# A ring of eight half size weight units, and six of them for token tile 0 ahead of tile 1

## The chip, the cores and the metric

The kernel runs on one core of one Trainium2 chip. The metric is the device time of one execution in microseconds (us); the number compared is the median of several runs.

## The reference

A transformer of three blocks on 256 tokens of width 1024, in float32. Everything is a chain of RMS norms, projections and small attentions:

```
h = x
layer 0: y = norm(h); y = [window attention (8 heads, rope, sinks) | HGRN2 (4 heads, blocks of 32)] @ w_out
layer 1: y = norm(h); y = chunk attention (16 heads, relative bias) @ w_out
both:    h = h + norm(y)
         y = (gelu(conv3(norm(h) @ w_u)) * (norm(h) @ w_v)) @ w_down      # 1024 -> 2816 -> 1024
         h = h + norm(y)
block 2: y = norm(h); three attentions of y (causal with rope; forgetting; over 256 memory rows)
         h = h + (sum of sigmoid(gate_b) * (attention_b @ w_b)) @ w_out
         h = h + (silu(norm(h) @ w_gate) * (norm(h) @ w_up)) @ w_down
```

The inputs of each projection are the whole output of the norm ahead of it, and each norm needs a full row (1024 features) of the projection ahead of it. There are 256 tokens, so each engine sees two tiles of 128 tokens, tile 0 and tile 1.

## The kernel before, in words

**Weights.** All weights are laid out on the host as 172 units of 128 partitions x 2048 columns (1 MB; UNIT = 2048, line 45; STREAM, line 49, lists the stages in their order with the number of units, the blocks of 128 input features in a unit and the columns). SyncE loads them in this order into a ring of RAW = 4 slots `raw` (line 411), waiting for the semaphore unit_used, which counts the units that TensorE has finished. ScalarE rounds each unit into `hi` (round_unit, line 508), VectorE subtracts to get the rest `lo` (split_unit, line 1136), and TensorE takes three products for each block: hi with the rounded activations, hi with their rest, lo with the rounded ones. So a unit passes through four engines: load, rounding, split, matmuls.

**Two kinds of product.** Token-major stages (tokens_by, tokens_unit; matmuls at line 790, 128 x 512) have 128 tokens as rows of PSUM, two banks a tile. A unit holds two blocks of 128 input features with 1024 columns, so a unit is 12 matmuls for tile 0 and 12 for tile 1. Feature-major stages (features_of; line 848, 128 x 256) have features as rows and both tiles as columns: q and k, the gates and the up projections. These need the activations of both tiles from the first matmul on.

**Order by hand.** Each engine's program is one fixed list. `units(n)` on ScalarE and VectorE means: round (split) all units up to n here. Whatever stands behind it in the list waits for it, and it waits for the load.

**The end of a projection and the next entry.** Six projections are TAILS: even_out, down0, odd_out, down1, merge_out, down2. Their last two units go as a pair: both units for tile 0 (then the semaphore tile_done), then both for tile 1. With tile_done VectorE and ScalarE begin on tile 0. norms_between is what they do behind the first four: the norm of the projection's output (weigh_product, square_product), its sum into h (add_product, line 1200), the squares and weights of the sum (square_sum, weigh), the scaling (scale, line 1181), then the transposed halves are rounded (turned_hi, line 546) and their rest taken (turned_lo, line 1187). GpSimd makes the reciprocal roots in between (lines 436 and 438). TensorE transposes the normed rows of a tile with `turn` (line 859), two semaphored halves of four transposes each.

On TensorE a token-major stage is entered by `enter`: turn tile 0, one unit for tile 0, turn tile 1 (`entry(1)`), the second unit for tile 0, then both units for tile 1. The feature-major up stages turn both tiles and then start. FEATURE_MAJOR (stages 3, 6 and 8) are up0, up1 and up2; stages 4 and 7 are odd_v and moba_qk; stages 2 and 5 are the entries to even_out and odd_out behind attentions; stage 0 is mem_kv. The core of VectorE's list between two norms:

```
weigh_product(g, 0, base, tile_done, ...)
units(last(name) + 1)
add_product(g, p, 0)
weigh(g + 1, 0, ...)
weigh_product(g, 1, base, unit_used, last(name))
scale(g + 1, 0)
```

Behind merge_out there is no norm of the product: add_residual (line 1231), squares, weigh, scale, turns.

Of the kernel before, what the change touches and what calls it, by code (L numbers as in the profile page):

```python
# [28 lines left out]
P = 128  # L29
S = 256  # L30
NT = S // P
D = 1024
KD = D // P
FF = 2816
# [10 lines left out]
UNIT = 2048  # L45
RAW = 4
# [3 lines left out]
    ("mem_kv", 4, 2, 1024),  # L50
    ("even_a", 4, 2, 768), ("even_qf", 4, 8, 256), ("even_ig", 4, 2, 1024), ("even_out", 4, 2, 1024),
    ("up0", 22, 8, 256), ("down0", 11, 2, 1024),
    ("odd_v", 4, 2, 1024), ("odd_qk", 8, 8, 256), ("odd_out", 4, 2, 1024),
    ("up1", 22, 8, 256), ("down1", 11, 2, 1024),
    ("moba_qk", 4, 2, 1024), ("both_v", 4, 2, 1024), ("fox_qk", 4, 2, 1024), ("mem_q", 3, 3, 520),
    ("gates", 12, 8, 256), ("branches", 6, 4, 512), ("merge_out", 4, 2, 1024),
    ("up2", 22, 8, 256), ("down2", 11, 2, 1024),
# [5 lines left out]
WIDTH[FIRST["mem_q"] + 2] = 2 * 520  # L63
# [12 lines left out]

TAILS = ["even_out", "down0", "odd_out", "down1", "merge_out", "down2"]
# [50 lines left out]
def lay_out(a):  # L128

    def rows(w, cols, k_of_unit):  # L130

        w = w[:, cols].reshape(-1, P, w[:, cols].shape[1])
        out = []
        for k0 in range(0, w.shape[0], k_of_unit):
            out.append(w[k0:k0 + k_of_unit].transpose(1, 0, 2).reshape(P, -1))
        return out

    def columns(w, groups):

        return [w[:, g].reshape(-1, P, len(g)).transpose(1, 0, 2).reshape(P, -1) for g in groups]  # L140

    r = np.arange
    pairs = [r(256 * j, 256 * j + 256) for j in range(4)]
    two = [np.concatenate([r(P * j, P * j + P), FF + r(P * j, P * j + P)]) for j in range(KF)]
    even, odd, w2 = a["even_w_in"][0], a["odd_w_in"][0], a["w_in_2"][0]
    u = rows(a["w_mem_kv_2"][0], r(1024), 2)

    heads = np.concatenate([r(HD * x, HD * x + HD) for p in range(4) for x in (p, 4 + p)] + [r(512, 768)])
    u += rows(even, heads, 2) + columns(even, [768 + g for g in pairs]) + rows(even, r(1792, 2816), 2)
    u += rows(a["even_w_out"][0], r(D), 2)  # L150
    u += columns(a["ffn_w_up"][0], two) + rows(a["ffn_w_down"][0], r(D), 2)
    u += rows(odd, r(2048, 3072), 2)
    u += columns(odd, [np.concatenate([r(P * j, P * j + P), D + r(P * j, P * j + P)]) for j in range(8)])
    u += rows(a["odd_w_out"][0], r(D), 2)
    u += columns(a["ffn_w_up"][1], two) + rows(a["ffn_w_down"][1], r(D), 2)
    u += rows(w2, r(1024), 2) + rows(w2, np.concatenate([r(1024, 1536), r(2560, 3072)]), 2)
    u += rows(w2, r(1536, 2560), 2) + rows(w2, r(3072, 3592), 3)
    u += columns(w2, [3592 + r(256 * j, 256 * j + 256) for j in range(12)])
    for name in ("w_br_moba_2", "w_br_fox_2", "w_br_mem_2"):
        u += columns(a[name][0], [r(512), r(512, 1024)])  # L160
    u += rows(a["w_out_2"][0], r(D), 2)
    gate_up = np.concatenate([a["w_gate_2"][0], a["w_up_2"][0]], 1)
    u += columns(gate_up, two) + rows(a["w_down_2"][0], r(D), 2)
# [22 lines left out]
def build(nc, dram, out):  # L186
    with ExitStack() as ctx:
# [133 lines left out]
        q_made = sem("q_made")  # L321
# [76 lines left out]
        def _(sp):  # L398
# [3 lines left out]
            for n in range(RAW):  # L402
                if n == 1:
                    sp.dma_start(mem_x[:, 1, :], dram["mem"][P:S, :]).then_inc(mem_in[1], 16)
                if n == 2:
                    sp.dma_start(h[:, :, :], dram["x"].rearrange("(t p) d -> p t d", p=P)).then_inc(x_in, 16)
                sp.dma_start(raw[:, n, :], dram["weights"][n]).then_inc(raw_in[n], 16)
            with sp.Fori(0, UNITS // RAW - 1) as i:
                for s in range(RAW):
                    sp.wait_ge(unit_used, RAW * i + s + 1)  # L410
                    sp.dma_start(raw[:, s, :], dram["weights"][RAW * i + (RAW + s)]).then_inc(raw_in[s], 16)
            for t in range(NT):
# [87 lines left out]
        def _(act):  # L500
# [75 lines left out]
            def feed_forward(layer):  # L576
# [8 lines left out]
                def tile(i, r):  # L585

                    j = 4 * i + r
                    act.wait_ge(unit_used, j + up + 1)
# [5 lines left out]
                    round_unit(j + up + 2, (up + 2 + r) % RAW, i + (up + 2 + r) // RAW, UNIT)  # L594
# [8 lines left out]
                done[0] += KF  # L603
# [4 lines left out]
            units(1)  # L608
            turned_hi(0, 4, h_hi, (0,))
            square_tokens(0, 1, mem_x, (mem_in[1], 16), (mem_in[1], 16))  # L610
            units(2)
# [5 lines left out]
            units(FIRST["even_a"] + 1)  # L617
# [3 lines left out]
            units(FIRST["even_a"] + 2)  # L621
# [3 lines left out]
            units(last("even_a") + 2)  # L625
# [3 lines left out]
            for u in range(4):  # L629
                act.wait_ge(unit_used, FIRST["even_qf"] + u + 1)  # L630
                dst = (hq if u < 2 else hf)[:, 2 * (u % 2):2 * (u % 2) + 2, :].rearrange("p a b -> p (a b)")
                act.activation(dst, bank(u), ACT.Copy if u < 2 else ACT.Sigmoid).then_inc(qf_evac, 1)
                units(FIRST["even_qf"] + u + 3)
            act.wait_ge(f_done, 1)
            act.activation(whole(hf), whole(hf), ACT.Ln).then_inc(ln_done, 1)
            units(FIRST["even_ig"] + 3)
# [3 lines left out]
            units(FIRST["even_ig"] + 4)  # L640
            act.wait_ge(last_done, 1)
            act.activation(whole(hf), whole(hf), ACT.Exp).then_inc(exp3_done, 1)
            units(last("even_ig") + 1)
# [3 lines left out]
            units(last("even_ig") + 2)  # L647
# [963 lines left out]
```

## Time and profile before

| what | value |
|---|---|
| median of 3 runs | 1204.79 us (1204.57 to 1205.15) |
| the profiled execution's own time | 1202.29 us |
| its span | 1200.5 us |
| mean granted TensorE clock | 0.95 |
| PE busy | 1137.8 us (95%), 7452 matmuls |
| weight loads of PE (PEld) | 1032.0 us |
| VectorE (DVE) busy | 703.0 us |
| ScalarE (ACT) busy | 537.6 us |
| GpSimd (POOL) busy | 83.3 us |
| moved by DMA | 194.17 MB, mean 162 GB/s |

PE is a matmul, PEld a weight load into the array, which runs beside the matmuls; SPq is SyncE's queue. A busy PE is not PE at its peak: its rate depends on the granted clock, 1.00 being 2.4 GHz and 0.50 being 1.2 GHz. The span is the part of the profiled execution between the first and the last instruction; 1.8 us of its time lie outside.

### The profile page before, as it was taken

The numbers are of one execution on the slowest core, as the hardware profiler recorded it, in microseconds if no ns is written. First come the engines' busy times: TensorE is split into PE (matmuls) and PEld (weight loads), VectorE is DVE, ScalarE is ACT, GpSimd is POOL, SyncE is SP. The second block draws the span as 40 slices with busy tenths as digits, with TensorE's granted clock in tenths as the row PEclk, the third lists the DMA queues.
The fourth block names the chain that finished last, engine by engine and source line by source line (L and its number), as shares of the span: only waits on it lengthen the run. The fifth ranks groups of instructions, "written<-read, shape, count | busy, mean of one in ns | idle before, by whom it ended". The sixth has DMA issues, their size and how long they took to land.

```text
span 1200.5 us, 18573 instructions
## 1 busy us (share of the span) xinstructions
PE 1137.8 (95%) x7452; PEld 1032.0 (86%) x7452; DVE 703.0 (59%) x937; ACT 537.6 (45%) x743; POOL 83.3 (7%) x113
## 2 busy tenths in 40 slices
PE   5999997999999899879999997999999998999998
PEld 4898676999987689769999886888999987999986
DVE  6567435666653556555666637556555575555542
ACT  5544324554543444434555434435544634444441
POOL 3200002000000201020000002203000000000000
PEclk9998577999999899889999998999999998999999
DMA  7854013555454454244555552554333353555552
GB/s 280 308 180 138 1 51 129 188 192 176 175 200 169 175 173 153 79 173 142 180 186 193 177 195 103 210 202 149 134 114 106 111 193 118 178 183 191 183 180 101
DMA packets 28876, 194.17 MB, mean 162 GB/s; under 512 B 3488, under 2 KB 3680, under 8 KB 6800
## 3 DMA queue, kind: packets, MB, share of 16 engines
q1 hardware_dynamic: 25760, 183.58, 43.9%
q0 software_dynamic: 3056, 9.73, 2.5%
q8 instruction: 45, 0.74, 0.2%
q14 instruction: 15, 0.12, 0.0%
HBM read 192.25 MB, written 1.05 MB: 161 GB/s over the span
## 4 chain that ended last, share of the span: by engine, by line
PE 88%; DVE 5%; ACT 3%; POOL 2%; issue 2%; DMA 1%; DVEq 0%; ACTq 0%; POOLq 0%
PE ps L848 46%; PE ps L790 31%; PE ps L929 3%; PE ps L906 2%; PE ps L859 2%; PE ps L918 1%; DVE xhat L1167 1%; DVE lo L1136 1%; POOL ms L436 1%; PE ps L875 1%; DMA gain<-in_gains 1%; PE ps L974 1%; DVE h L1200 1%; ACT hi L508 1%; DVE y_lo L1187 1%
## 5 line engine op out<-in xcount | busy, mean ns | idle before, releaser
L1136 DVE TENSOR_TENSOR lo<-raw,hi 128x2048 fp32r<-128x2048 f32 (+2 forms) x172 | 389.1, 2266 | 166.9 <-ACT hi L508 166.8
L848 PE MATMUL ps<-y_hi,hi 128*128 128x256 f32 x1504 | 431.2, 287 | 2.0 <-DVE y_lo L1187 2.0
L848 PE MATMUL ps<-y_lo,hi 128*128 128x256 f32 x1504 | 428.4, 285 | 0.0
L848 PE MATMUL ps<-y_hi,lo 128*128 128x256 f32 x1504 | 428.3, 285 | 0.0
L508 ACT ACTIVATE hi<-raw 128x2048 fp32r<-128x2048 f32 (+2 forms) x172 | 323.5, 1887 | 137.3 <-DMA raw<-in_weights 131.2
L848 PEld LDWEIGHTS ps<-y_hi,hi 128*128 128x128 f32 x1504 | 291.5, 194 | 4.1 <-issue 3.7
L848 PEld LDWEIGHTS ps<-y_lo,hi 128*128 128x128 f32 x1504 | 291.6, 194 | 0.0
L848 PEld LDWEIGHTS ps<-y_hi,lo 128*128 128x128 f32 x1504 | 291.3, 194 | 0.0
L790 PE MATMUL ps<-hi,h_hi 128*128 128x512 f32 x328 | 102.6, 394 | 2.0 <-DVE h_lo L1187 1.2
L790 PE MATMUL ps<-hi,h_lo 128*128 128x512 f32 x328 | 102.6, 394 | 0.0
L790 PE MATMUL ps<-lo,h_hi 128*128 128x512 f32 x328 | 102.1, 393 | 0.0
L790 PE MATMUL ps<-hi,y_hi 128*128 128x512 f32 (+2 forms) x288 | 91.6, 399 | 3.1 <-DVE y_lo L1187 2.2
L790 PE MATMUL ps<-lo,y_hi 128*128 128x512 f32 (+2 forms) x288 | 88.9, 390 | 0.0
L790 PE MATMUL ps<-hi,y_lo 128*128 128x512 f32 (+2 forms) x288 | 88.1, 387 | 0.0
L590 ACT ACTIVATE sc<-ps,conv 128x256 f32<-128x256 f32 x44 | 24.9, 565 | 131.3 <-PE ps L848 131.3
L790 PEld LDWEIGHTS ps<-hi,h_hi 128*128 128x128 f32 x328 | 61.5, 189 | 16.6 <-DVE h_lo L1187 1.6
L790 PEld LDWEIGHTS ps<-hi,h_lo 128*128 128x128 f32 x328 | 61.9, 189 | 13.5
L790 PEld LDWEIGHTS ps<-lo,h_hi 128*128 128x128 f32 x328 | 61.9, 189 | 13.3
L859 PE MATMUL ps<-ident,xhat 128*128 128x128 f32 x144 | 29.5, 374 | 44.0 <-DVE xhat L1181 41.6
L790 PEld LDWEIGHTS ps<-hi,y_hi 128*128 128x128 f32 x288 | 54.9, 198 | 16.0 <-DVE y_lo L1187 3.8
L436 POOL TENSOR_SCALAR ms<-ss 128x1 f32<-128x1 f32 x22 | 20.0, 909 | 686.6 <-ACT sc L528 651.5
L859 PEld LDWEIGHTS ps<-ident,xhat 128*128 128x128 f32 x144 | 24.1, 193 | 49.1 <-DVE xhat L1181 34.4
(237 smaller groups left out, 1046.2 us busy)
## 6 DMA issues: line engine op xcount, KB each, us to landing
raw<-in_weights SPq DMA_DIRECT2D x172, 1024.0 KB, 4.8
gain<-in_gains POOLq DMA_DIRECT2D x11, 512.0 KB, 5.4
bias<-in_rel POOLq DMA_DIRECT2D x16, 128.0 KB, 2.4
mem_x<-in_mem SPq DMA_DIRECT2D x2, 512.0 KB, 6.8
h<-in_x SPq DMA_DIRECT2D x1, 1024.0 KB, 13.9
out<-h SPq DMA_DIRECT2D x2, 512.0 KB, 2.6
pick<-in_c_pick POOLq DMA_DIRECT2D x1, 512.0 KB, 8.0
head_gain<-in_head_gains POOLq DMA_DIRECT2D x1, 256.0 KB, 7.9
```

The lines of the kernel that those rows point to most:

```text
L436: pool.tensor_scalar(ms[:, g % 2, t:t + 1], ss[:, g % 2, t, 0:1], ss[:, g % 2, t, 1:2], EPS, ALU.add, ALU.add).then_inc(scaled_ms, 1)
L508: act.activation(hi[:, s, :w], raw[:, s, :w], ACT.Copy).then_inc(hi_done, 1)
L590: act.activation(sc[:, r % 2, :S], ps[:, r, :S], ACT.Identity, scale=conv[:, layer, j, 2:3], bias=conv[:, layer, j, 3:4]).then_inc(conv_be ...
L790: mm = pe.matmul(ps[:, base + 2 * t + half_, :cw], x[:, k + kk, tok], w[:, n % RAW, kk * cols + c0:kk * cols + c0 + cw], start=first and k ...
L848: mm = pe.matmul(dst, w[:, s % RAW, at], x(k), start=first and k == 0, stop=final and k == nk - 1)
L859: mm = pe.transpose(ps[:, base + 2 * t + kh, kk * P:(kk + 1) * P], src[:, t, (4 * kh + kk) * P:(4 * kh + kk + 1) * P], ident[:, :])
L875: mm = pe.transpose(ps[:, b, kk * P:(kk + 1) * P], src[:, t, c0 + kk * P:c0 + (kk + 1) * P], ident[:, :])
L906: mm = pe.matmul(dst, q[:, t * P:(t + 1) * P], k[:, :n], start=True, stop=stage != "f")
L918: mm = pe.transpose(ps[:, 2 + a % 2, i * P:(i + 1) * P], pr[:, a % 2, i * P:(i + 1) * P], ident[:, :])
L929: mm = pe.matmul(place(stage, hh, t), pt[:, a % 2, i * P:(i + 1) * P], v(kt), start=kt == 0, stop=kt == kts[-1])
L974: mm = pe.matmul(ps[:, 5 + b % 3, hh * P:(hh + 1) * P], kend[r, b // 4, hh * P:(hh + 1) * P], hv[r, b // 4, hh * P:(hh + 1) * P], start=Tr ...
L1136: dve.tensor_tensor(lo[:, s, :w], raw[:, s, :w], hi[:, s, :w].bitcast(F32), ALU.subtract).then_inc(lo_done, 1)
```

## The change

It has four parts.

1. Units are half as wide and the ring has twice as many slots: UNIT = 1024, RAW = 8. A token-major unit is now one block of 128 input features with 1024 columns, 6 matmuls a tile; a feature-major one is 128 columns for all 8 blocks. 344 units; every wait counts in half units.
2. At the end of each of the six tails, six half units go for tile 0 and then six for tile 1 (TAIL = 6; before, two whole ones, four halves). At the entries to odd_v and moba_qk six half units go for tile 0 before tile 1 (LEAD = 6); mem_kv has four, even_out and odd_out two, being what their tails leave of eight.
3. `turn_next`: the transposes of tile 0 for the next stage are issued on TensorE ahead of the last half part of tile 1 of the projection, no longer behind it. In a lead, tile 1 is turned ahead of tile 0's last half part.
4. ScalarE's and VectorE's lists between two norms are put in another order, and the feed forward tile rounds and splits one half unit ahead of and one behind its Gelu and product.

The core of the diff:

```diff
-UNIT = 2048
-RAW = 4
+UNIT = 1024
+RAW = 8
+LEAD, TAIL = 6, 6
...
# TensorE, tokens_by
+                def by_tile(first, count, leads, is_tail):
+                    for n in range(first, first + count):
+                        wait_unit(n)
+                        if needs is not None:
+                            pe.wait_ge(*needs(n - n0))
+                        if leads and n == n0 + 4:
+                            pe.wait_ge(y_lo_done, 4 * stage + 2)
+                        if leads and n == first + count - 1:
+                            entry(1)
+                        mm = part(n, 0)
+                    if is_tail:
+                        mm.then_inc(tile_done, 1)
+                    for n in range(first, first + count):
+                        if leads and n - n0 in (0, 4):
+                            pe.wait_ge(y_lo_done, 4 * stage + 3 + (n - n0) // 4)
+                        if is_tail and n == last(name) - 1:
+                            turn_next()
+                        part(n, 1).then_inc(unit_used, 1)
...
+                lead = 4 if name == "mem_kv" else n1 - n0 - TAIL if name in TAILS else LEAD
...
# VectorE, norms_between
                 dve.wait_ge(turned, 4 * stage)
+                units(last(name) + 2)
                 weigh_product(g, 0, base, tile_done, TAILS.index(name) + 1)
-                units(last(name) + 1)
                 add_product(g, p, 0)
                 weigh(g + 1, 0, [h[:, 0, 0:512], h[:, 0, 512:D]])
+                scale(g + 1, 0)
+                units(last(name) + 4)
+                turned_lo(stage, turn_base, y_lo, y_hi, (0,))
                 weigh_product(g, 1, base, unit_used, last(name))
-                scale(g + 1, 0)
...
+                add_product(g, p, 1)
+                weigh(g + 1, 1, [h[:, 1, 0:512], h[:, 1, 512:D]])
+                if stage not in FEATURE_MAJOR:
+                    units(last(name) + 5)
+                scale(g + 1, 1)
+                if stage not in FEATURE_MAJOR:
+                    units(last(name) + 6)
+                turned_lo(stage, turn_base, y_lo, y_hi, (1,))
...
# ScalarE, norms_between
-                units(last(name) + 1)
+                units(last(name) + 2)
                 square_product(g, 0, base, tile_done, TAILS.index(name) + 1)
-                units(last(name) + 2)
                 square_sum(g + 1, 0, p)
+                units(last(name) + 4)
+                turned_hi(stage, turn_base, y_hi, (0,))
                 square_product(g, 1, base, unit_used, last(name))
-                turned_hi(stage, turn_base, y_hi, (0,))
+                if stage not in FEATURE_MAJOR:
+                    units(last(name) + 5)
                 square_sum(g + 1, 1, p)
+                if stage not in FEATURE_MAJOR:
+                    units(last(name) + 6)
                 turned_hi(stage, turn_base, y_hi, (1,))
...
# VectorE, behind merge_out
             add_residual("merge_out", 4, 0)
             weigh(10, 0, [h[:, 0, 0:512], h[:, 0, 512:D]])
-            units(last("merge_out") + 1)
+            scale(10, 0)
+            units(last("merge_out") + 2)
+            turned_lo(8, 4, y_lo, y_hi, (0,))
             add_residual("merge_out", 4, 1)
-            scale(10, 0)
             weigh(10, 1, [h[:, 1, 0:512], h[:, 1, 512:D]])
-            turned_lo(8, 4, y_lo, y_hi, (0,))
+            units(last("merge_out") + 4)
             scale(10, 1)
             turned_lo(8, 4, y_lo, y_hi, (1,))
...
# ScalarE, behind merge_out
             square_sum(10, 0, 4)
-            units(last("merge_out") + 1)
+            units(last("merge_out") + 2)
+            turned_hi(8, 4, y_hi, (0,))
             square_sum(10, 1, 4)
-            turned_hi(8, 4, y_hi)
-            units(last("merge_out") + 2)
+            units(last("merge_out") + 4)
+            turned_hi(8, 4, y_hi, (1,))
...
# ScalarE, feed forward tile (VectorE alike)
-                    round_unit(j + up + 2, (up + 2 + r) % RAW, i + (up + 2 + r) // RAW, UNIT)
+                    round_unit(n + 4, m % RAW, i + m // RAW, UNIT)
                     ... Gelu or Silu ...
+                    round_unit(n + 5, (m + 1) % RAW, i + (m + 1) // RAW, UNIT)
```

In odd_qk, q and k are half units of their own, so q's copy waits for unit_used in place of q_made, and in `tokens_by` merge_out waits for the second half of its input after its fourth half unit.

## Rows read from the trace of the kernel before

**Rows 1.** The page: parts 1 and 4.
```profile
PE 1137.8 (95%) x7452; PEld 1032.0 (86%) x7452; DVE 703.0 (59%) x937; ACT 537.6 (45%) x743; POOL 83.3 (7%) x113
...
PE 88%; DVE 5%; ACT 3%; POOL 2%; issue 2%; DMA 1%; DVEq 0%; ACTq 0%; POOLq 0%
```
**Rows 2.** Waits of PE: line waited for: us in total, times, longest.
```profile
PE ps L859 <- DVE xhat L1181: 41.6, 11, 11.3
```
**Rows 3.** Windows: length, busy us of each engine, clock, DMA share, GB/s.
```profile
188.00:191.60 3.60, 0.03 (x1) 0.00 (x0) 3.57 (x7) 2.76 (x8) 1.30 (x3) 1.00 1.00 380
403.80:406.30 2.50, 2.50 (x8) 2.02 (x7) 1.39 (x2) 2.38 (x3) 1.68 (x4) 0.50 0.95 311
205.00:329.00 124.00, 124.00 (x1034) 124.00 (x1033) 82.08 (x104) 63.59 (x84) 0.00 (x0) 1.00 0.52 178
```
**Rows 4.** The chain that ended last: start us, us, what.
```profile
106.17 1.43 ACT hi L508
...
329.25 54.95 PE ps L790 x240
...
404.15 20.40 PE ps L790 x84
```
**Rows 5.** Groups by form: busy us, mean ns, idle before.
```profile
L1136 DVE TENSOR_TENSOR lo<-raw,hi 128x2048 fp32r<-128x2048 f32 x165 | 377.2, 2291 | 162.0 <-ACT hi L508 161.9
L508 ACT ACTIVATE hi<-raw 128x2048 fp32r<-128x2048 f32 x165 | 313.6, 1907 | 133.0 <-DMA raw<-in_weights 126.9 <-PE ps L848 6.1
...
L1187 DVE TENSOR_TENSOR y_lo<-ps,y_hi 128x512 fp32r<-128x512 f32 x32 | 21.5, 689 | 29.9 <-ACT y_hi L546 29.7
...
L1136 DVE TENSOR_TENSOR lo<-raw,hi 128x1536 fp32r<-128x1536 f32 x4 | 7.0, 1755 | 1.6 <-ACT hi L508 1.6
...
L508 ACT ACTIVATE hi<-raw 128x1536 fp32r<-128x1536 f32 x4 | 6.0, 1495 | 1.4 <-DMA raw<-in_weights 1.4
```
**Rows 6.** Timeline, even_out to up0: start us, length us, operation, idle before.
```profile
182.73 1.37 DVE L1167 TENSOR_TENSOR xhat<-ps,gain 128x512 f32<-128x512 f32 x2 [6.75 <-PE ps L790]
...
189.88 1.28 DVE L1167 TENSOR_TENSOR xhat<-ps,gain 128x512 f32<-128x512 f32 x2
...
191.61 1.82 PE L859 MATMUL ps<-ident,xhat 128*128 128x128 f32 x8 [3.58 <-DVE xhat L1181]
...
192.78 1.41 DVE L1200 SCALAR_TENSOR_TENSOR h<-xhat,rstd,h 128x512 f32<-128x512 f32 x2 [0.83 <-POOL rstd L438]
193.47 0.60 ACT L546 ACTIVATE y_hi<-ps 128x512 fp32r<-128x512 f32 x1 [0.26 <-PE ps L859]
...
199.83 0.55 PE L848 MATMUL ps<-y_hi,hi 128*128 128x256 f32 x1 [0.65 <-DVE y_lo L1187]
```
**Rows 7.** Timeline, down0 to odd_v.
```profile
384.32 1.37 DVE L1167 TENSOR_TENSOR xhat<-ps,gain 128x512 f32<-128x512 f32 x2 [7.39 <-PE ps L790]
...
398.64 1.41 DVE L1200 SCALAR_TENSOR_TENSOR h<-xhat,rstd,h 128x512 f32<-128x512 f32 x2
...
402.23 0.88 DVE L1181 TENSOR_SCALAR xhat<-xhat,rstd 128x512 f32<-128x512 f32 x2 [0.84 <-POOL rstd L438]
...
402.77 1.38 PE L859 MATMUL ps<-ident,xhat 128*128 128x128 f32 x8 [2.05 <-DVE xhat L1181]
```
**Rows 8.** Timeline, merge_out to up2.
```profile
992.54 1.29 DVE L1231 TENSOR_TENSOR h<-ps,h 128x512 f32<-128x512 f32 x2 [6.77 <-PE ps L790]
...
993.96 0.61 ACT L528 ACTIVATE sc<-h 128x512 f32<-128x512 f32 x1
...
1003.66 0.87 DVE L1181 TENSOR_SCALAR xhat<-xhat,rstd 128x512 f32<-128x512 f32 x2
...
1006.81 0.55 PE L848 MATMUL ps<-y_hi,hi 128*128 128x256 f32 x1 [0.65 <-DVE y_lo L1187]
```
**Rows 9.** The page's DMA issues: KB each, median us to landing.
```profile
raw<-in_weights SPq DMA_DIRECT2D x172, 1024.0 KB, 4.8
...
out<-h SPq DMA_DIRECT2D x2, 512.0 KB, 2.6
```

More of the change, by code:

```diff
@@ L43 @@
 REL = 128
-UNIT = 2048
-RAW = 4
+UNIT = 1024
+RAW = 8
 STREAM = [
[L50 to L57, printed above, removed]
+    ("mem_kv", 8, 1, 1024),
+    ("even_a", 8, 1, 768), ("even_qf", 8, 8, 128), ("even_ig", 8, 1, 1024), ("even_out", 8, 1, 1024),
+    ("up0", 44, 8, 128), ("down0", 22, 1, 1024),
+    ("odd_v", 8, 1, 1024), ("odd_qk", 16, 8, 128), ("odd_out", 8, 1, 1024),
+    ("up1", 44, 8, 128), ("down1", 22, 1, 1024),
+    ("moba_qk", 8, 1, 1024), ("both_v", 8, 1, 1024), ("fox_qk", 8, 1, 1024), ("mem_q", 8, 1, 520),
+    ("gates", 24, 8, 128), ("branches", 12, 4, 256), ("merge_out", 8, 1, 1024),
+    ("up2", 44, 8, 128), ("down2", 22, 1, 1024),
 ]
@@ L62 @@
     WIDTH += [_k * _c] * _n
-WIDTH[FIRST["mem_q"] + 2] = 2 * 520
 UNITS = len(WIDTH)
@@ L128, in lay_out, with rows, columns @@
 def lay_out(a):
[L130 to L140, printed above, removed]
+    def rows(w, cols):
+        return list(w[:, cols].reshape(-1, P, len(cols)))
+    def columns(w, cols, width=P):
+        return [w[:, cols[c:c + width]].reshape(-1, P, width).transpose(1, 0, 2).reshape(P, -1) for c in range(0, len(cols), width)]
@@ L154, in lay_out @@
[L154 to L158, printed above, removed]
+    u = rows(a["w_mem_kv_2"][0], r(1024))
+    u += rows(even, heads) + columns(even, 768 + r(1024)) + rows(even, r(1792, 2816)) + rows(a["even_w_out"][0], r(D))
@@ L675, in _ @@
             norms_between(4, 1, 4, "down0", 4, 0)
-            units(last("odd_v") + 2)
+            units(last("odd_v") + 4)
             act.wait_ge(unit_used, last("odd_v"))
@@ L793, in tokens_unit, with tokens_by @@
                 return mm
-            def tokens_by(name, base, y, splits=((0, 512), (512, 512)), entry=None, ready=None, before_last=lambda: None, needs=None):
+            def tokens_by(name, base, y, splits=((0, 512), (512, 512)), entry=None, stage=None, before_last=lambda: None, needs=None, turn_next=lambda: None):
                 n0, n1 = FIRST[name], last(name)
-                first_k = [sum(WIDTH[n0:n]) // COLS[name] for n in range(n0, n1)]
                 def part(n, t):
-                    return tokens_unit(name, n, first_k[n - n0], t, base, y, splits)
-                def pair(n, between=lambda: None, halfway=lambda mm: None):
-                    wait_unit(n)
-                    part(n, 0)
-                    between()
-                    wait_unit(n + 1)
-                    halfway(part(n + 1, 0))
-                    for m in (n, n + 1):
-                        if ready is not None and m == n0:
-                            pe.wait_ge(*ready)
-                        part(m, 1).then_inc(unit_used, 1)
-                n = n0
-                if entry is not None:
-                    pair(n, lambda: entry(1))
-                    n += 2
-                    pe.wait_ge(ready[0], ready[1] + 1)
-                tail = n1 - 2 if name in TAILS else n1
@@ L822, in tokens_by @@
+                n = n0
+                lead = 4 if name == "mem_kv" else n1 - n0 - TAIL if name in TAILS else LEAD
+                if stage is not None and lead:
+                    by_tile(n, lead, True, False)
+                    n += lead
+                    pe.wait_ge(y_lo_done, 4 * stage + 4)
+                tail = n1 - TAIL if name in TAILS else n1
                 while n < tail:
-                    if n == n1 - 1:
+                    if n == n1 - 2:
                         before_last()
@@ L1003, in _, with feed_forward @@
             pe.wait_ge(mk_evac, 2)
-            enter(2, 4, "even_out", 0, attended, [2, 2])
-            def feed_forward(layer, stage, base):
+            enter(2, 4, "even_out", 0, attended, [2, 2], turn_next=lambda: turn_normed(3, 4, 0))
+            def feed_forward(layer, stage, base, turn_next=lambda: None):
                 up = FIRST[f"up{layer}"]
-                for t in range(NT):
-                    turn(stage, xhat, base, t, normed, 2 * NORM_OF_TURN[stage] + t + 1)
+                turn_normed(stage, base, 1)
                 def tile(i, r):
@@ L1444, in _ @@
             units(last("even_out"))
-            norms_between(2, 0, 0, "even_out", 3, 4, 2)
+            norms_between(2, 0, 0, "even_out", 3, 4)
             feed_forward(0)
-            norms_between(4, 1, 4, "down0", 4, 0, 3)
-            units(last("odd_v") + 2)
+            norms_between(4, 1, 4, "down0", 4, 0)
+            units(last("odd_v") + 4)
             dve.wait_ge(unit_used, last("odd_v"))
```

256 lines of the change are left out of this document (125 added, 131 removed).

## The prediction

> **What bounds the kernel now.** I read the page first, then PE's waits, then the order of time at the turns from one stage to the next, then the operations by form. TensorE carries 88% of the chain that ended last [rows 1], so only what PE waits for, or what slows PE, can move the time. Of its waits one group matters: the transposes of the normed rows wait for VectorE's scaling, 41.6 us in 11 waits [rows 2], 11.3 of it at the kernel's start. They stand at five places: behind even_out and odd_out (then an up stage, which needs both token tiles), behind down0 and down1 (then odd_v and moba_qk, which can start on tile 0), and behind merge_out. The loads, rounding and splitting of the weights have room: in an up stage PE is busy all 124 us while VectorE is at 82, ScalarE at 64 and the DMA engines at 0.52 [rows 3]. So the sum is made at the five places, and the rest of the ring is weighed only for what it puts in the chain.
>
> **Units of time.** A matmul of 512 columns takes 0.229 us (54.95 us for 240 [rows 4]). A half unit for one tile (a part) is 6 of them, 1.37 us. The change sends tile_done 6 parts before the end of a projection (8.24 us) instead of 4 (5.50 us). Below, T is where PE would end the projection if it never stalled, and times with a plus sign count from tile_done, so T is +5.50 before and +8.24 after.
>
> **Half size operations.** From 1536 to 2048 columns the split grows from 1755 to 2291 ns and the rounding from 1495 to 1907 ns [rows 5]. A line through each pair gives 1.22 us for a split of 1024 columns and 1.08 us for a rounding; two halves cost 0.15 and 0.26 us more than one whole. That is 25 and 45 us over 172 units, hidden behind PE as long as the engines have the room shown above. It shows only where a rounding or split stands in the chain, as the ScalarE rounding at 106.17 us does [rows 4]. The chain has some three such pieces away from the five places: 3 x 0.26, about +0.7 us.
>
> **even_out to up0, odd_out to up1.** Before: VectorE starts on tile 0's product at 182.73, so tile_done is at 182.69; PE turns tile 0 at 191.61 (+8.92), and its first up matmul is at 199.83 [rows 6]. That is T + 11.6. After: the two splits moved ahead of tile 0's product are done before tile_done (their ring slots come free when the tail begins, 8.2 us earlier), so tile 0's chain is as long as before. PE comes to the point of turn_next after 5 parts, at +6.87, and has to wait until about +8.8: **a stall of 1.9 us ahead of the last part** that wasn't there. Eight transposes (0.9) and the last part (1.37) then end at about +11.1, at T + 2.8. Meanwhile VectorE: the scaling ends at +9.2; then two splits stand ahead of turned_lo, 2 x 1.22, to +11.6; turned_lo of tile 0, two operations of the 0.67 us kind [rows 5], to +12.9. Only then does it take tile 1's product, 1.8 us after PE has it ready. From that start to the first up matmul it was 189.88 to 199.83, 9.95 us [rows 6]; there tile 1's squares stood 0.3 us behind tile 0's y_hi copy (193.47 to 194.07, where the sums are ready from 193.5 on), which goes, so 9.6. The up stage starts at +22.5, which is T + 14.3: **2.6 us later, twice, +5.2 us**. Bounds: were the two splits free, the chain would start at +11.1 and the loss were 0.8; were the last part at half clock, +0.5 on top of 2.6, since VectorE is then only just late.
>
> **down0 to odd_v, down1 to moba_qk.** Before: tile_done at 384.28, T at 389.78, and odd_v ends with a run of 84 matmuls at 404.15 + 20.40 = 424.55, T + 34.8 [rows 4, 7]. After, the start is as above; y_lo's first half is there at +12.3 and PE goes on with parts 0 to 3 of tile 0, to +17.8. Part 4 needs its unit split, and that split stands behind tile 1's product (+12.9), its residual sum (2.90 us after that start [rows 6], +15.8, 1.41 long) and the weighing (1.4): from +18.6 to +19.8. Root and scaling: the scaling comes 3.59 us after the sum's start at the earliest (398.64 to 402.23 [rows 7]), +19.4, so the split binds and the scaling runs +19.8 to +20.7. Then the sixth unit's split, to +21.9. The order on PE asks for that unit before entry(1), so tile 1 is turned at +21.9 to +22.9, and part 5 follows. 11 of 16 parts are left: 15.1 us, end at +38.0, T + 29.8. The gain is 5.0 us. Two short stalls (2.0 and 0.7 us) may let the clock fall: after the 2.05 us ahead of the turn at 402.77 [rows 7] PE ran at 0.50 for 2.5 us [rows 3]; that costs up to 1.3 us, of which I take 0.5, since the stretch at half clock can as well fall on parts 0 to 3, which have 2 us of slack. **4.5 us gained, twice, -9.0 us**; bounds 2.5 and 5.3. If the cover (the lead of six parts while tile 1's norm runs) were gone, the gain would be about 1 us each.
>
> **merge_out to up2.** No product norm here, so tile 0's chain is short. Before: sums start 992.54, tile_done 992.50, first up matmul 1006.81 [rows 8], T + 8.8. After: rows scaled at about +4.5, so PE does not stall at +6.87; turn and last part end at +9.1. Tile 1's sum starts at +9.2, its squares end 2.1 us later (992.54 to 994.66 with the accumulator read [rows 8]), +11.3; now ScalarE's two roundings follow (+13.5), VectorE's last split (+14.7), and only then the scaling, 3.15 us before the first matmul (1003.66 to 1006.81 [rows 8]): +17.9, T + 9.6. **+0.8 us**; bounds 0 (splits early) and +1.5.
>
> **The rest.** even_out and odd_out are entered with two half units in place of two whole ones; tile 1 is ready in both, and the turn moves to between parts 0 and 1: 0, bounds -0.3 and +1. mem_kv: the same bytes come in the same order, and the third part's wait for its split cancels against the earlier start: 0, bounds -1 and +1. The feed forward loops have the rounding and split in two with the Gelu between: hidden (above). SP issues 344 loads in place of 172. A load of 1024 KB lands after 4.8 us, a store of 512 KB after 2.6 [rows 9], and with several loads in flight the queue moved 380 GB/s [rows 3]; an up stage needs 178, and the ring holds as many bytes as before. I take 0, with half loads between 2.6 and 4.8 us.
>
> The Trainium skill, DMA: Bandwidth & Descriptors, section "Bandwidth", says to batch transfers to 1 MiB or more to get three quarters of the peak, which speaks against halving the loads; by its fixed 2.0 us plus bytes over 436 GB/s (section on the SWDGE path) a half load takes an estimated 3.2 us. Taken one at a time such loads would bring 164 GB/s, less than an up stage takes. The trace's 380 GB/s with loads in flight says that they overlap.
>
> **The sum.** 5.2 - 9.0 + 0.8 + 0.7 = -2.3 us. The profiled execution took 1202.29 us, 2.5 below the median of 1204.79; its span would fall from 1200.5 to 1198.2. Laid on the median: **1202.4 us**.
>
> **Rivals.**
> 1. As forecast, mixed: the two starts on tile 0 win, the three up stages lose. 1202.4, own range 1200.5 to 1204.3. 45%.
> 2. The hold costs the up stages nearly nothing: roundings and splits slip into VectorE's gaps. For it: VectorE idles 3 us while the root is made. Against: its order is written out, the splits stand behind the scaling. Then 2 x 0.8 in place of 5.2 and 5.3 won twice: 0.7 + 1.6 + 0.5 - 10.6 = -7.8, up to the forecast; centre 1198.5. 15%.
> 3. The clock takes the difference: at each of four holds PE stalls twice more, and parts and leads run at 0.50 for 2.5 us [rows 3], 1.3 us each on the two token stages' path, 0.5 on the others': about +3, so 1205. Against: the clock stayed at 1.00 through an idle 3.6 us [rows 3]. 20%.
> 4. Slower, by one mechanism: **the wait for tile 0's rows ahead of the last part**. If that wait is longer than 1.9 us because ScalarE or VectorE reach tile_done late (the two units now ahead of the product must have landed, been rounded and split within 8.2 us), everything behind moves with it one for one, at four places. Needed are a load of at most 4.8, a rounding of 1.08 and a split of 1.22, 7.1 together, so 1.1 us are in hand. It decides from about 1.2 us of lateness at each (4 x 1.2 = 4.8, twice the forecast's gain); with 2 us at four places: -2.3 + 8 = 1210.5, with 1 us 1206.5. 13%.
> 5. The lead starves: parts 4 and 5 wait longer for their splits than I work out, and the leads gain 2 us each instead of 4.5: 1207. 5%.
> 6. Half loads don't overlap: 164 GB/s against 178 in three up stages, 5.75 us a whole unit becoming 6.4 for 66 units, +43 us: 1245. 2%. That is what the rule above would give at its worst.
>
> **How the numbers follow.** What a measurement tells from no change here is about 0.2%, 2.4 us. Of the forecast's 45 somewhat over half lies below 1202.4 and its like; with rival 2 that makes 0.43 faster. Rival 3 and the other part of the forecast: 0.40. Rivals 4 to 6: 0.17 slower, less a little. The range leaves out 1 in 10 at each end: 1197.0 to 1207.0.
>
> **What would show it.** Idle PE of about 1.9 us directly ahead of the transposes, with one part behind them, at 4 places and none at merge_out; first up matmul 22.5 us after tile_done; two splits of about 1.22 us between tile 0's scaling and its y_lo; in odd_v 5 parts of tile 0, then the transposes, about +21.9. Wrong would be: tile 1's product taken as soon as PE ends, splits absent from that gap, a tile_done chain longer than 8.9 us, or PE waiting for a weight load in an up stage.

## The result: 1.3% faster, and the profile after

| | before | after |
|---|---|---|
| median, same chip | 1204.68 us (1201.9 to 1205.15, 4 runs) | 1187.9 us (1186.8 to 1188.9, 4 runs) |
| ratio | | 0.987, 95% interval 0.985 to 0.988 |
| profiled execution, its span | 1202.29, 1200.5 us | 1188.9, 1187.1 us |
| mean granted clock | 0.95 | 0.959 |

In a second set of runs the change gave 0.988 (0.986 to 0.989). The forecast was 1202.4 with a range of 1197.0 to 1207.0: the time lies 9 us below its lower end.

The page of after, parts 1, 4 and 6 (against [rows 1, 9]):
```profile
PE 1125.4 (95%) x7452; PEld 1022.4 (86%) x7452; DVE 714.5 (60%) x1111; ACT 560.1 (47%) x917; POOL 76.4 (6%) x113
PE 88%; DVE 4%; ACT 3%; DMA 2%; POOL 1%; issue 1%; SPq 0%; ACTq 0%; DVEq 0%
raw<-in_weights SPq DMA_DIRECT2D x346, 512.0 KB, 3.5
```
There are 346 half units, not 344 as I wrote: mem_q had three units and has eight now. GpSimd was busy 83.3 us and is now 76.4 for the same 113 instructions. That is the row that I had not thought about.

PE's waits of after (against [rows 2]), and the window of the up stage and that of odd_v's lead (against [rows 3]):
```profile
PE ps L863 <- DVE xhat L1193: 33.5, 4, 10.4
PE ps L788 <- DVE lo L1148: 3.3, 3, 1.3
PE ps L863 <- DVE lo L1148: 2.2, 2, 1.1
```
```profile
205.00:329.00 124.00, 124.00 (x1026) 123.59 (x1025) 83.43 (x129) 69.72 (x110) 0.00 (x0) 1.00 0.53 182
396.00:400.00 4.00, 2.36 (x12) 1.75 (x13) 2.48 (x4) 0.01 (x1) 3.92 (x8) 1.00 0.34 90
```
The waits for the scaled rows fell from 11 to 4, their sum from 41.6 to 33.5 us: the four that are left are at the start and ahead of tile 1's turn in the three up stages. In odd_v PE now waits a little for splits (1.26 and 1.12 us), and the clock stays at 1.00 where before it stood at 0.50 [rows 3].

After, even_out to up0 (against [rows 6]):
```profile
177.82 1.40 DVE L1179 TENSOR_TENSOR xhat<-ps,gain 128x512 f32<-128x512 f32 x2
179.40 0.30 POOL L428 TENSOR_SCALAR ms<-ss 128x1 f32<-128x1 f32 x1 [49.06 <-ACT sc L520]
...
184.59 1.09 PE L863 MATMUL ps<-ident,xhat 128*128 128x128 f32 x8
184.85 1.22 DVE L1148 TENSOR_TENSOR lo<-raw,hi 128x1024 fp32r<-128x1024 f32 x1
...
186.22 1.22 DVE L1148 TENSOR_TENSOR lo<-raw,hi 128x1024 fp32r<-128x1024 f32 x1 [0.15 <-ACT hi L500]
187.36 1.28 DVE L1199 TENSOR_TENSOR y_lo<-ps,y_hi 128x512 fp32r<-128x512 f32 x2
188.56 1.28 DVE L1179 TENSOR_TENSOR xhat<-ps,gain 128x512 f32<-128x512 f32 x2
...
197.91 0.55 PE L852 MATMUL ps<-y_hi,hi 128*128 128x256 f32 x1 [0.65 <-DVE y_lo L1199]
```
tile_done is at 177.78. The turn comes at +6.8 with no idle time ahead of it, where I had +8.8 and a stall of 1.9. Everything behind keeps my distances to within 0.4 us: product of tile 1 at +10.8 (forecast 12.9), first up matmul at +20.1 (22.5).

The same place before, rows that I had not read:
```profile
184.02 2.28 DVE L1136 TENSOR_TENSOR lo<-raw,hi 128x2048 fp32r<-128x2048 f32 x1
184.30 2.16 POOL L436 TENSOR_SCALAR ms<-ss 128x1 f32<-128x1 f32 x1 [52.95 <-ACT sc L528]
186.55 0.57 POOL L438 TENSOR_TENSOR rstd<-ms,half 128x1 f32<-128x1 f32 x1
```
A GpSimd operation on one number a partition took 2.16 us and ended with the split on VectorE; in after the same operation takes 0.30. It is the first step of the root of tile 0's norm, in the middle of the chain that I had called "as long as before". The change moved the split ahead of the product, out of its way.

After, down0 to odd_v (against [rows 7]), and the chain (against [rows 4]):
```profile
389.99 1.27 DVE L1179 TENSOR_TENSOR xhat<-ps,gain 128x512 f32<-128x512 f32 x2
...
394.92 1.63 POOL L428 TENSOR_SCALAR ms<-ss 128x1 f32<-128x1 f32 x1 [2.43 <-ACT pr L520]
395.25 1.22 DVE L1148 TENSOR_TENSOR lo<-raw,hi 128x1024 fp32r<-128x1024 f32 x1
...
397.23 0.88 DVE L1193 TENSOR_SCALAR xhat<-xhat,rstd 128x512 f32<-128x512 f32 x2 [0.76 <-POOL rstd L430]
```
```profile
326.69 54.95 PE ps L788 x240
400.39 14.99 PE ps L788 x66
```
odd_v ends at 415.38, 9.2 us earlier than before; 2.6 of them were there when down0 began. The split at 395.25 holds GpSimd again (1.63 us), as the change placed it so.

Lengths of the five turns in each profile, in us, from the chain's pieces of PE: even_ig's end to the first up0 matmul; down0's start to odd_v's end; from there to the first up1 matmul; down1's start to the end of mem_q (moba_qk's turn is in it); from there to the first up2 matmul.

| kernel | up0 | odd_v | up1 | moba_qk | up2 | median |
|---|---|---|---|---|---|---|
| before | 94.8 | 95.3 | 114.0 | 155.5 | 183.7 | 1203.0 to 1204.7 |
| after | 93.9 | 88.7 | 116.6 | 148.7 | 184.0 | 1187.9 |
| after, again | 94.2 | 88.4 | 116.6 | 148.6 | 184.0 | 1188.9 |
| split ahead, in before | 93.1 | 91.4 | 113.2 | 153.1 | 184.8 | 1197.8 |
| one split behind | 95.0 | 89.0 | 116.5 | 149.1 | 184.1 | 1190.7 |
| both behind | 96.4 | 90.1 | 116.3 | 150.1 | 184.1 | 1193.1 |
| turn behind | 95.2 | 88.5 | 116.4 | 148.5 | 185.4 | 1191.5 |
| tail of 4 | 97.0 | 90.9 | 118.0 | 151.0 | 185.4 | 1201.0 |
| lead of 4 | 94.8 | 92.4 | 116.4 | 152.6 | 184.1 | 1196.2 |
| ring only | 96.8 | 92.2 | 118.4 | 152.3 | 185.5 | 1201.9 |
| late up splits | 93.0 | 88.6 | 113.0 | 148.7 | 182.2 | 1184.2 |
| + turn first | 93.4 | 87.8 | 114.5 | 147.6 | 182.2 | 1183.5 |
| + fifth split early | 93.7 | 88.0 | 113.2 | 147.7 | 182.2 | 1183.1 |

What stands ahead of the first column varies from one profile to the next where its code is the same (the second run of matmuls starts at 58.2 to 61.3 us), so the columns say more than the spans.

The columns up0 and up1 also hold what PE does ahead of the norm: an attention and the entry to even_out or odd_out. The next table cuts them at T, the prediction's point (tile_done, 0.04 us ahead of the first start on tile 0, plus 8.24 us, or plus 5.50 with a tail of four). "From T" ends where the column ends. What is ahead of T is 60.5 us in odd_v and moba_qk in every kernel.

| kernel | up0, ahead of T | up1, ahead of T | up0, from T | odd_v, from T | up1, from T | up2, from T |
|---|---|---|---|---|---|---|
| before | 83.1 | 102.4 | 11.7 | 34.8 | 11.6 | 8.8 |
| forecast | | | 14.3 | 29.8 | 14.3 | 9.6 |
| after | 82.0 | 104.0 | 11.9 | 28.2 | 12.6 | 9.5 |
| after, again | 82.4 | 104.0 | 11.8 | 27.9 | 12.5 | 9.5 |
| split ahead, in before | 82.0 | 102.5 | 11.1 | 30.9 | 10.7 | 8.4 |
| both behind | 82.9 | 102.8 | 13.5 | 29.6 | 13.5 | 9.5 |
| turn behind | 83.0 | 104.0 | 12.2 | 28.1 | 12.4 | 10.8 |
| late up splits | 82.5 | 102.6 | 10.5 | 28.1 | 10.5 | 7.6 |

The forecast's 29.8 leaves out the 0.5 that it allowed for the clock. Ahead of T the same code gives 82.0 to 83.0 and 102.6 to 104.0 us, so up to 1.5 us of a column is no work of the edit; from T on the repetition agrees to 0.4. What differs ahead of T in up1 is how long the clock stood at 0.50 at the entry to odd_out. The transposes of tile 1 there, before and after:
```profile
506.87 0.87 PE ps L859 x8
```
```profile
496.92 1.71 PE ps L863 x8
```

### The profile page after: what moved, and what is told of

The parts are those of the page before. It is cut to its first block, busy times and chain, and to the rows that moved or that the text cites. A ratio compares the mean times of both kernels' runs of the same rounds, so it can differ in the third digit from the quotient of the medians.

```text
span 1187.1 us, 19769 instructions
## 1 busy us (share of the span) xinstructions
PE 1125.4 (95%) x7452; PEld 1022.4 (86%) x7452; DVE 714.5 (60%) x1111; ACT 560.1 (47%) x917; POOL 76.4 (6%) x113
## 4 chain that ended last, share of the span: by engine, by line
PE 88%; DVE 4%; ACT 3%; DMA 2%; POOL 1%; issue 1%; SPq 0%; ACTq 0%; DVEq 0%
PE ps L852 46%; PE ps L788 31%; PE ps L936 3%; PE ps L913 3%; DMA raw<-in_weights 2%; DVE lo L1148 2%; PE ps L925 1%; PE ps L863 1%; ACT hi L500 1%; DVE y_lo L1199 1%; ACT pr L520 1%; POOL ms L428 1%; PE ps L882 1%; PE ps L990 0%; POOL rstd L430 0%
## 5 line engine op out<-in xcount | busy, mean ns | idle before, releaser
L1148 DVE TENSOR_TENSOR lo<-raw,hi 128x1024 fp32r<-128x1024 f32 (+2 forms) x346 | 409.7, 1204 | 115.1 <-ACT hi L500 114.3
L500 ACT ACTIVATE hi<-raw 128x1024 fp32r<-128x1024 f32 (+2 forms) x346 | 350.2, 1036 | 123.3 <-DMA raw<-in_weights 115.5
L788 PE MATMUL ps<-hi,h_hi 128*128 128x512 f32 x328 | 102.8, 395 | 3.9 <-DVE h_lo L1199 2.5
L788 PE MATMUL ps<-hi,h_lo 128*128 128x512 f32 x328 | 102.5, 394 | 0.0
L788 PE MATMUL ps<-hi,y_hi 128*128 128x512 f32 (+2 forms) x288 | 87.9, 386 | 6.1 <-DVE y_lo L1199 3.6
L788 PE MATMUL ps<-lo,y_hi 128*128 128x512 f32 (+2 forms) x288 | 86.3, 380 | 0.0
L1317 DVE SCALAR_TENSOR_TENSOR sc<-ps,conv,sc 128x255 f32<-128x255 f32 x44 | 21.2, 483 | 86.9 <-ACT sc L587 86.9
L788 PEld LDWEIGHTS ps<-lo,y_hi 128*128 128x128 f32 x288 | 53.7, 190 | 10.5
L788 PEld LDWEIGHTS ps<-hi,y_lo 128*128 128x128 f32 x288 | 53.5, 190 | 10.5
```

What stands on the lines that cost most here:

```text
L500: act.activation(hi[:, s, :w], raw[:, s, :w], ACT.Copy).then_inc(hi_done, 1)
L788: mm = pe.matmul(ps[:, base + 2 * t + half_, :cw], x[:, k, tok], w[:, n % RAW, c0:c0 + cw], start=first and k == 0, stop=final and n == la ...
L1148: dve.tensor_tensor(lo[:, s, :w], raw[:, s, :w], hi[:, s, :w].bitcast(F32), ALU.subtract).then_inc(lo_done, 1)
L1317: dve.scalar_tensor_tensor(c[:, 1:S], ps[:, r, 0:S - 1], conv[:, layer, j, 1:2], c[:, 1:S], ALU.mult, ALU.add).then_inc(dve_link, 1)
```

## The experiments

**1. In before, only VectorE's split moved ahead of tile 0's product.**
```diff
-                weigh_product(g, 0, base, tile_done, ...)
                 units(last(name) + 1)
+                weigh_product(g, 0, base, tile_done, ...)
```


> The kernel before with one edit: VectorE's split of the next stage's first unit stands ahead of tile 0's product instead of behind it, at the four turns with a product norm. ScalarE's rounding of the second unit stays beside GpSimd's operation. Theory A (VectorE's split, with two operands in SBUF, holds up GpSimd's root): the first GpSimd operation of each turn (L436) falls from 2.16 to 0.3 us, tile 0 is turned about 1.9 us earlier, and the kernel gains some 1.5 to 1.9 us at each of the four, 6 to 7.5 in all. Theory B (the 2.16 us is a slow first operation after a long pause of GpSimd, or ScalarE's rounding beside it): it stays 2.16 and the time stays the same within 1 us.

1197.8 us, ratio 0.995 (0.994 to 0.996), 5.5 us won by one exchange of lines.
```profile
180.74 2.29 DVE L1136 TENSOR_TENSOR lo<-raw,hi 128x2048 fp32r<-128x2048 f32 x1 [5.90 <-ACT hi L508]
182.95 1.28 DVE L1167 TENSOR_TENSOR xhat<-ps,gain 128x512 f32<-128x512 f32 x2
184.52 0.30 POOL L436 TENSOR_SCALAR ms<-ss 128x1 f32<-128x1 f32 x1 [53.18 <-ACT sc L528]
```
The root's first step is 0.30 us at all four places. In even_out the unit's load is late, so the product waits for the split (182.95, where PE was done by 181.6), and in odd_out by 1.0 us too; that is why the up stages win 0.6 and 0.9 us from T on and not 1.9. odd_v wins 3.9, more than the root has to give: the rest comes with the clock, which is 1.00 here from 398 to 404 us, past tile 1's turn, and was 0.50 behind that turn before [rows 3]. So the 5.5 us are the split's place with what the clock made of it, less the late loads.

**2 and 3. In after, one or both half splits put back behind the product.**
```diff
-                units(last(name) + 2)
+                units(last(name) + 1)      # one behind; both behind: none here
                 weigh_product(g, 0, ...)
+                units(last(name) + 2)
```


> The changed kernel with one of the two half unit splits that it does ahead of tile 0's product put behind it. Theory A: GpSimd's first operation takes 1.1 us instead of 0.30, PE stalls 0.8 us ahead of the last part at four turns, +0.8 us each, +3.2 in all. Theory B: GpSimd's operation stays 0.30 and nothing is lost, 0 within 1 us.

> The changed kernel with both half unit splits behind tile 0's product, the place that the whole unit had before. Theory A: GpSimd's operation is held through both splits, 2.1 to 2.2 us; +1.9 us at four turns, about +7.5 us, and PE stalls 1.9 us ahead of the last part, which is what the prediction worked out. If GpSimd gets in between the two, 1.1 us and +3.2 in all. Theory B: 0 within 1 us.

1190.7 us (ratio 0.989, 0.988 to 0.991) and 1193.1 (0.991, 0.990 to 0.993). The changed kernel was not in this set; by its two ratios it would stand at 1187.4 to 1188.5, so one split behind costs 2.2 to 3.3 us (3.2 expected) and both cost 4.6 to 5.7 (7.5 expected). One split behind:
```profile
179.54 1.22 DVE L1148 TENSOR_TENSOR lo<-raw,hi 128x1024 fp32r<-128x1024 f32 x1
179.80 1.13 POOL L428 TENSOR_SCALAR ms<-ss 128x1 f32<-128x1 f32 x1 [49.53 <-ACT sc L520]
```
Both behind:
```profile
179.79 2.35 DVE L1148 TENSOR_TENSOR lo<-raw,hi 128x1024 fp32r<-128x1024 f32 x2
180.08 2.15 POOL L428 TENSOR_SCALAR ms<-ss 128x1 f32<-128x1 f32 x1 [49.93 <-ACT sc L520]
...
187.12 1.10 PE L863 MATMUL ps<-ident,xhat 128*128 128x128 f32 x8 [1.96 <-DVE xhat L1193]
```
0.30, 1.13, 2.15: the wait goes with the splits, and two back to back don't let GpSimd in between. With both, the predicted stall of 1.9 us ahead of the last part is there (1.96), and the first up matmul is 21.7 us after tile_done (forecast 22.5). At the norms this behaves as the kernel that I forecast. It costs less than 4 x 1.9 because in after VectorE does not use all of the time won: tile 1's product comes 1.6 us sooner at even_out but only 1.0 at odd_out, where the second split in the gap waits 0.83 us for its rounding.

**4. In after, tile 0 turned behind the last part again.**

> The changed kernel with tile 0's next transposes issued behind the last part of tile 1, not ahead of it. Theory A: PE comes to that place at +6.87 us and tile 0's rows are ready at +6.85, so turning ahead costs no stall, and what it brings is hidden by the loads of the third and fourth half unit: 0 within 1 us. Rival C (turning early is what gained): 0.9 to 1.4 us lost at each of five turns, +4.5 to +7.

1191.5 us (0.989, 0.988 to 0.991), some 3 to 4 more than the changed kernel would have in this set: neither 0 nor the rival's 4.5 and more. From T on up2 loses 1.4 us and up0 0.3, the other three nothing; 1.0 of up0's column and the rest of the profile's difference lie elsewhere, where the code is the same. So what is shown of turn_next is 1.6 us, nearly all at merge_out, and little at the norms of a product, where VectorE and not PE is late.

**5. The changed kernel again.**

> The changed kernel as it is, again, as the measure for the others of this group: 1187.9 us, 0.987 of before. If the chip of this group gives another ratio, the others are to be compared with this one.

1188.9 us, 0.988 (0.986 to 0.989): the measure for 6 to 8.

**6. Tail of four half units** (`LEAD, TAIL = 6, 4`).

> The changed kernel with four half units at the end of each tail in place of six (tile_done 5.5 us ahead of the end in place of 8.2). Theory (the norm chain of tile 0 now takes 6.8 us to the turn and VectorE is free for tile 1's product at +10.8): PE reaches the turn at +4.1 and stalls 2.7 us ahead of the last part, and VectorE takes tile 1's product at T + 5.3 in place of T + 2.6. Both say +2.7 us at each of four turns, and +1 at merge_out at most: 11 us more than the changed kernel, about 1199. Rival (the gain came from the ring of smaller units, not from the longer tail): within 2 us of the changed kernel.

1201.0 us (0.998, 0.997 to 0.999), 12.1 more. The stall ahead of the last part is 2.80 us:
```profile
188.91 1.09 PE L863 MATMUL ps<-ident,xhat 128*128 128x128 f32 x8 [2.80 <-DVE xhat L1193]
```
**7. Lead of four** (`LEAD, TAIL = 4, 6`).

> The changed kernel with four half units in place of six for tile 0 at the entries to odd_v and moba_qk. PE then has 5.5 us of work in place of 8.2 while tile 1's norm and turn run. From the trace of the changed kernel (tile 1 turned at +20.4, and parts 0 to 4 of tile 0 end about +17): with four parts PE stops at +15.3 before tile 1's turn, and the two parts lost are 2.7 us less of cover, of which up to 1.5 us was slack. Theory: 1.2 to 2.7 us later at each of two places, +2.4 to +5.4 in all, 1190 to 1193. Rival (the splits of the fifth and sixth half unit hold up tile 1's norm as much as they cover): no difference, within 1 us.

1196.2 us (0.993, 0.992 to 0.994), 7.3 more: above my range. PE idles 3.96 us ahead of tile 1's turn, and then runs the turn and what follows at 0.50, which I had not counted:
```profile
399.33 1.94 PE L863 MATMUL ps<-ident,xhat 128*128 128x128 f32 x8 [3.96 <-DVE xhat L1193]
```
```profile
400.00:404.00 4.00, 4.00 (x13) 3.38 (x13) 3.21 (x4) 3.08 (x4) 1.96 (x4) 0.50 0.98 320
```
The turns of odd_v and moba_qk are 4.0 us longer each. The lead's two extra parts cover the idle time and keep the clock.

**8. The ring alone** (4 and 4, turn behind the last part).

> The changed kernel with four half units in place of six at tails and entries (as many bytes as before the change) and tile 0 turned behind the last part: what is left is the ring of half units and the new order of the lists. Theory: the tail of four costs what it cost alone, +12; the lead of four another +8 less what overlaps; only turning behind the last part costs nothing at the four turns, since VectorE and not PE is late there, and +1.4 at merge_out. About 1208 (1203 to 1211), not faster than before, though GpSimd's root is quick (0.30 us) here as in the changed kernel. Rival (the ring and the order carry the gain, the six are an extra): 1195 to 1200.

1201.9 us (0.999, 0.998 to 1.000): no faster than before, 6 us less than I expected. Missed was that the losses overlap: the turns come out as with the tail of four, and the lead of four adds 1.3 us at each of two places, not 4, since tile 1's chain, late already, sets the end. GpSimd's quick root is in it, and still it is 4 us slower than before with its split moved (experiment 1), which has as many bytes at tails and entries, whole units and the old order. In the old order VectorE took tile 1's product 6.7 us after tile_done at even_out, here 10.6. So the two splits ahead of tile 1's product are the likely loss; no run separates the order from the half size units, and the old order with the split ahead and a tail of six was not tried.

**9. Late splits for the up stages, in after.**
```diff
+                if stage not in FEATURE_MAJOR:
                     units(last(name) + 4)
                 turned_lo(stage, turn_base, y_lo, y_hi, (0,))
...
                 turned_lo(stage, turn_base, y_lo, y_hi, (1,))
+                units(last(name) + 4)
...                                        # ScalarE alike, and both engines behind merge_out
```


> The changed kernel with the rounding and split of the third and fourth half unit of the three up stages moved behind tile 1's y_hi and y_lo, so VectorE takes tile 1's product (and behind merge_out the scaling) without two splits of 1.22 us ahead of it. At up0 and up1 the product is then taken when PE has it, +9.2 in place of +10.8: -1.6 us each. At up2 two roundings and two splits leave the chain of tile 1's scaling: -1 to -2. The first up matmuls need only the two half units already split, 6.6 us of work at full clock for each... the third's rounding and split, 2.3 us, stand then behind y_lo beside them. Theory: 4 to 5 us less than the changed kernel, 1183 to 1184. Rival (the late splits stop PE at the third half unit, or the root is slowed again by a split that moved): the gain is given back, within 1 us of the changed kernel.

1184.2 us (0.983, 0.982 to 0.985), 4.7 less than after. At up0 and up1:
```profile
187.37 1.29 DVE L1200 TENSOR_TENSOR y_lo<-ps,y_hi 128x512 fp32r<-128x512 f32 x2 [0.98 <-ACT y_hi L538]
188.57 1.47 DVE L1180 TENSOR_TENSOR xhat<-ps,gain 128x512 f32<-128x512 f32 x2
...
526.54 1.97 PE L864 MATMUL ps<-ident,xhat 128*128 128x128 f32 x8 [6.79 <-DVE xhat L1194]
```
Tile 1's product is taken at +9.3 from the tile_done at 179.2, and PE's idle time ahead of tile 1's turn at up1 is 6.79 us, where the changed kernel has 8.88 (there the second split in the gap had also waited for its load). From T on up0 wins 1.3, up1 2.1 and up2 1.9 us. A half unit of an up stage is 2.9 us of work (128.8 us for 44), not the 6.6 that I expected, and it was enough. This is the one of my steps that cost the up stages most (two splits in the gap), here taken away.

**10. Also tile 1's turn ahead of the wait for the sixth split.**
```diff
-                        wait_unit(n)
-                        ...
                         if leads and n == n0 + 4:
                             pe.wait_ge(y_lo_done, 4 * stage + 2)
                         if leads and n == first + count - 1:
                             entry(1)
+                        wait_unit(n)
+                        ...
```


> The kernel with late splits ahead of the up stages (1184.2), and in the leads tile 1 is turned before PE waits for the sixth unit's split, no longer behind that wait. In the trace of the changed kernel the scaled rows of tile 1 are ready at 397.23 and PE turns at 399.30, when the split is done. Theory: the turn comes about 1.5 us sooner, the next thing in line is the sixth split (done at the same time as before) and then tile 1's y_lo; 0.9 us of transposes go from the path at each of two places, -1.8 us, 1182.4. Rival (tile 1's y_lo, behind the sixth split on VectorE, sets the end anyway): 0.

1183.5 us (0.983, 0.982 to 0.985). Odd_v and moba_qk are 0.8 and 1.0 us shorter, as expected, and up1 1.5 longer in this profile, all of it ahead of T (104.1 against 102.6 us), where the code is the same; against experiment 9 the time is not told apart.

**11. Also the fifth split ahead of tile 1's product.**

> As the kernel with the turn ahead of the wait, and the fifth unit's rounding and split go ahead of tile 1's product (from behind its weighing, where the split holds GpSimd's root for 1.63 in place of 0.58 us). Theory: the split's 1.22 us move from one place of the chain to another, the root gets 1.05 us quicker, and PE has the fifth part ready without the idle 1.3 us: 1 us less at each of two places, about 1180.5. Rival (its load lands only 1 to 2 us behind the end of the projection, and everything of tile 1 now waits for it): +1 to +2 at each, 1184 to 1186.

1183.1 us (0.983, 0.982 to 0.985), the least of all, though 9 to 11 can't be told apart. The root's step falls from 1.63 to 0.58 us, and the turns don't get shorter (88.0 against 87.8): the product waits as long for the split as the root did.

**12. What of VectorE's operation holds GpSimd.** Both behind, as in 3, but `tensor_copy(lo, raw)` in place of the subtraction, which this kernel leaves out for the eight units.

> The changed kernel with the two half units that stood ahead of tile 0's product put behind it, as in the experiment before (there GpSimd's root operation took 2.15 us), but made by a copy with one input in place of the subtraction of two; so the subtraction is left out for these eight units. It tells what of VectorE's operation holds GpSimd. Theory by rows: the operations with two inputs from SBUF held it to their end. If it is the second input, the root operation beside the copies takes 0.30 to 0.58 us. If it is any long operation of VectorE, it takes until the copies end, 1 us or more.

1189.5 us in its one run.
```profile
179.05 1.28 DVE L1221 CAST lo<-raw 128x1024 fp32r<-128x1024 f32 x2
179.34 1.08 POOL L428 TENSOR_SCALAR ms<-ss 128x1 f32<-128x1 f32 x1 [49.52 <-ACT sc L520]
```
The operation ends with the second copy here too, so the second input is not the only cause. One copy took 0.64 us where the subtraction took 1.22. The Trainium skill, SBUF — State Buffer, section "SBUF: two separate sides", says that VectorE and GpSimd share a pair of ports that is taken whole by whoever starts first, VectorE needing it in its fast two-port mode, or with two inputs from SBUF against a GpSimd operation that reads SBUF. The trace agrees that both kinds hold GpSimd (2.15 and 1.08 us against 0.30); that the copy ran in the two-port mode it doesn't show, only that it was the faster one. That ScalarE's rounding doesn't hold GpSimd is seen in experiment 1, where one ran beside the 0.30. Whoever starts first is not what decided between two operations back to back: in experiment 3 GpSimd's record begins at 180.08, ahead of the second split, and yet ends with it.

## Why the prediction was wrong

**The step that failed first:** the two splits are done before tile_done, "so tile 0's chain is as long as before". The splits were indeed done. But the chain, which I put at 8.8 us to the turn, took 6.8: it held a duration that was set by the split's place, 2.16 us of GpSimd in before and 0.30 in after. With the splits put back it is 8.7 us, and that costs 4.6 to 5.7 us of the time (experiment 3); the split moved alone in before brings 5.5, part of it by the clock (experiment 1). The step also drew the stall of 1.9 us, rival 4's ground, into the forecast; it wasn't there.

**The two starts on tile 0** were forecast at -4.5 us each and gave -6.6 and -6.9. With GpSimd held as before (both behind) they gave -5.2 and -5.4: the direction and most of the size were right. Of the rest, 0.5 is the half clock that I allowed for and that did not come: PE's idle pieces of 1.3, 1.3 and 1.1 us left the clock at 1.00. Experiment 7 shows what the lead is worth by that: 4.0 us each, not 2.7.

**The two up stages** were forecast at +2.6 each. Their columns gave -0.8 and +2.6, and the second is a hit by luck: from T on, where the forecast was made, they gave +0.2 and +0.9. The rest is -1.1 and +1.6 ahead of T, the clock at the entries, which varies as much where the code is the same. With both behind, from T on, they gave +1.9 each, so with the chain as long as I had it 0.7 of each 2.6 was sized high. Two splits in the gap ahead of tile 1's product were right as a mechanism: taking them out (experiment 9) brought 1.3 and 2.1 us from T on, where I had put their cost at 1.8.

**merge_out** was forecast at +0.8 and gave +0.4 (+0.7 from T on), and its late splits were the reason given: without them (experiment 9) the turn is 1.9 us shorter.

**The rest** was forecast at +0.7 and gave -2.0: the start and the up loops (129.42 us before, 128.78 after, 128.99 in the repetition), each within what same code varies by. I found no +0.7 for the half size operations.

**The sum in spans:** forecast -2.3, measured -13.4. Of the 11.1 missing, 5.1 are the root (after against both behind, summed over the five columns), 3.3 the terms of the turns that I had sized high by up to 0.9 each, 2.7 the rest, which no run tells from chance. The medians lie 16.8 apart in the first set and 14.4 in the second; the profile of before was a quick one, 2.5 us below its median.

**Of the rivals,** 2 (the hold costs the up stages nearly nothing, 1198.5) was nearest in sign and gave the wrong reason: the hold costs what I said, and the chain got shorter. 3 and 4 did not come, nor 5 and 6: half loads land in 3.5 us, and an up stage takes them at 182 GB/s without a wait. What the change is made of: six at the tail 12.1 us, six in the lead 7.3, the turn ahead 1.6 by the turns and 3 to 4 by the medians, the ring and the new order together nothing that counts (1201.9 against 1203.0). These overlap, so their sum (21 and more) is more than the whole (14.4).

## What to carry to other kernels

Before a chain is taken to be "as long as before", compare the durations of its small operations on GpSimd: a 128x1 operation that takes 2 us is waiting inside its own record, and the row beside it on VectorE with the same end says for what. The wait list doesn't show it, since it counts as busy. Place wide VectorE operations where no root is being made, then ask at each place which engine is late: PE (turn earlier), VectorE (splits later), or the clock (more work in the gap).

## What the runs showed of the hardware that I had not expected

- GpSimd's 128x1 operation: 0.30 us alone, 0.58 beside the end of the weighing, 1.13 beside one 1024-column split, 1.63 beside a weighing and a split, 2.15 beside two splits or one of 2048 columns, 1.08 beside two copies.
- Loads of half the size landed in 3.5 us in place of 4.8 (the prediction's estimate was 3.2), and where several were in flight they moved 382 GB/s, as the whole ones had [rows 3]. In after:
```profile
408.00:412.00 4.00, 4.00 (x19) 3.34 (x18) 2.51 (x3) 2.21 (x3) 0.00 (x0) 1.00 1.02 382
```
- The clock stayed at 1.00 through idle pieces of PE of 1.96 us (experiment 3) and 2.80 us (experiment 6) ahead of the turn in even_out, and was at 0.50 after 2.05 [rows 7] and 3.96 us. In the kernel of experiment 1 it was at 0.50 in odd_v from 392 to 396 us, after pieces of 1.96 and 0.98 us. So the length of one idle piece did not decide it.
